# Sample attention of a hybrid encoder layer: four 32-row products on row groups of their own, scanned running sums, one turn for rotary keys

## The reference

```python
def fox_attend(q, k, v, cum_q, cum_k, qpos, kpos):
    s = jnp.einsum('bqhd,bkhd->bhqk', q, k).astype(jnp.float32) * FOX_SCALE
    s = s + jnp.swapaxes(cum_q, 1, 2)[..., :, None] - jnp.swapaxes(cum_k, 1, 2)[..., None, :]
    ...
def mla_attend(q_lat, q_rope, ckv, krope, qpos, kpos):
    s = (jnp.einsum('bqhc,bkc->bhqk', q_lat, ckv) + jnp.einsum('bqhr,bkr->bhqk', q_rope, krope)).astype(jnp.float32) * MLA_SCALE
    ...
    # sample_layer
    cum = jnp.cumsum(jnp.concatenate([c_logf.astype(jnp.float32), logf], axis=1), axis=1)
    fox_o = fox_attend(fq, k_all, v_all, cum[:, past:], cum, qpos, kpos)
```

## Time and profile before

| | us |
|---|---|
| median of 3 runs | 1612.63 (1611.25 to 1615.20) |
| profiled execution | 1609.14 |
| its span, first to last instruction | 1606.9 |
| TensorE busy in it | 1536.9 (96%) |
| VectorE, ScalarE busy | 630.9 (39%), 286.5 (18%) |
| mean granted TensorE clock | 0.988 of full speed |

### The profile page before, as it was taken

The page is one execution under the profiler, slowest core; times in us unless marked ns, Lnnn a source line. Parts: engine busy times, 40 slices in busy tenths (PEclk is TensorE's granted clock), DMA queues, the critical chain, the costliest instruction groups (busy, mean ns, idle before and its releaser), DMA issues.

```text
span 1606.9 us, 20794 instructions
## 1 busy us (share of the span) xinstructions
PE 1536.9 (96%) x7759; PEld 741.6 (46%) x7760; DVE 630.9 (39%) x1232; ACT 286.5 (18%) x617; POOL 37.7 (2%) x43
## 2 busy tenths in 40 slices
PE   6999999999999888999999999999999999999996
PEld 4876566656786563333333333333333333333332
DVE  2246444002123464344353443533533533533535
ACT  1125444210002321111111110110110110110111
POOL 0000000000004200000000000000000000000000
PEclk9999999999999979999999999999999999999999
DMA  9413145832333366399999999999999999999994
GB/s 271 134 37 111 51 196 190 286 105 96 127 105 130 114 262 243 143 403 417 417 419 417 417 419 417 417 420 417 417 420 416 418 419 416 418 419 417 418 419 201
DMA packets 125384, 481.15 MB, mean 299 GB/s; under 512 B 20048, under 2 KB 47984, under 8 KB 90400
## 3 DMA queue, kind: packets, MB, share of 16 engines
q1 hardware_dynamic: 112832, 471.79, 74.1%
q0 software_dynamic: 2016, 6.49, 1.1%
q10 hardware_dynamic: 10496, 2.32, 0.8%
HBM read 475.52 MB, written 4.65 MB: 299 GB/s over the span
## 4 chain that ended last, share of the span: by engine, by line
PE 66%; DMA 16%; SPq 11%; DVE 3%; issue 2%; ACT 1%; DVEq 0%; ACTq 0%
PE bank L463 61%; DMA ring<-in_w_gu 16%; SPq L1174 7%; SPq L1177 4%; PE bank L1092 1%; PE bank L775 1%; PE bank L1141 1%; PE bank L477 1%; PE bank L828 0%; DMA xr<-in_x_sample 0%; PE bank L786 0%; DVE small L1435 0%; PE bank L711 0%; SPq L1194 0%; DVE ring L1446 0%
## 5 line engine op out<-in xcount | busy, mean ns | idle before, releaser
L463 PE MATMUL bank<-ring,latent 128*64 128x512 f32 (+2 forms) x3328 | 745.1, 586 | 15.9 <-DMA ring<-in_w_gu 15.9
L463 PEld LDWEIGHTS bank<-ring,latent 128*64 128x64 f32 (+1 forms) x3328 | 250.7, 139 | 481.4 <-issue 413.6
L1717 DVE TENSOR_SCALAR latent<-bank 128x512 f32<-128x512 f32 x33 | 22.8, 692 | 509.8 <-PE bank L463 509.8
L1701 DVE TENSOR_TENSOR xr<-xr,bank 128x512 f32<-128x512 f32 x204 | 128.1, 683 | 44.1 <-PE bank L463 44.1
L463 PE MATMUL bank<-latent,fkT 64*128 64x512 f32 x408 | 135.0, 624 | 0.7 <-ACT latent L2054 0.7
L463 PE MATMUL bank<-hT,ring 128*128 128x384 f32 x384 | 124.5, 487 | 1.0 <-DVE hT L1328 1.0
L463 PE MATMUL bank<-ring,hT 128*128 128x256 f32 (+1 forms) x528 | 110.5, 371 | 0.0
L463 PEld LDWEIGHTS bank<-ring,hT 128*128 128x128 f32 x528 | 96.2, 190 | 13.5 <-issue 0.9
L2047 ACT ACTIVATE probTs<-latent 128x512 f32<-128x512 f32 x33 | 20.8, 630 | 455.9 <-DVE latent L1717 455.9
L463 PE MATMUL bank<-heads,latent 128*64 128x512 f32 x408 | 95.0, 601 | 1.9 <-issue 1.9
L463 PEld LDWEIGHTS bank<-hT,ring 128*128 128x128 f32 x384 | 72.8, 190 | 51.5 <-issue 1.5
(11 more groups left out here) (310 smaller groups left out, 1119.0 us busy)
## 6 DMA issues: line engine op xcount, KB each, us to landing
ring<-in_w_gu SPq DMA_DIRECT2D x256, 1024.0 KB, 19.7
ring<-in_w_down SPq DMA_DIRECT2D x128, 1024.0 KB, 21.0
ring<-in_w_in SPq DMA_DIRECT2D x16, 1024.0 KB, 11.0
ring<-in_cache_fox_k SPq DMA_DIRECT2D x8, 1024.0 KB, 4.8
ring<-in_cache_fox_v SPq DMA_DIRECT2D x8, 1024.0 KB, 7.4
ring<-in_cache_mla_ckv SPq DMA_DIRECT2D x8, 512.0 KB, 5.6
ring<-in_w_out SPq DMA_DIRECT2D x4, 1024.0 KB, 5.1
ring<-in_cache_mem_k SPq DMA_DIRECT2D x8, 512.0 KB, 3.3
```

The lines of the kernel that those rows point to most:

```text
L463: return pe.matmul(o, l, r, start=start, stop=stop, skip_group_check=True)
L1701: v.tensor_tensor(x, x, psum[5 + i % 3][:, :], ALU.add).then_inc(shares_added, 1)
L1717: v.tensor_scalar(gS, gate[:, :], LIMIT, None, ALU.min).then_inc(gate_clipped, 1)
```

## The change

- The forget product has 32 rows instead of 64: `sel4` covers 4 requests, `cumS` has two halves of 4 requests at partitions 64 to 95, and `cumN` lies apart at 96 to 127. The rotary queries are kept twice, at partitions 0 to 31 and 32 to 63.
- `sample_scores` opens four banks at once and issues the four 32-row products first, on four row groups. `("sN", b)` is split in `("sNf", b)` and `("sNm", b)`; the wait for the copy of the rotary keys comes first.
- `cumS` is made by four turns of `lgc`, interleaved by k so that a row holds the tokens in order, and two running sums on VectorE (`tensor_tensor_scan`). `cumN` takes one product with `lgsum`, which VectorE sums up before. The constant shrinks from 1024 to 384 columns. As cumS now lies in token order, the forget product reads it at every fourth word.
- The rotary keys of a request are turned once, 128x128, instead of four times 128x32, and ScalarE takes them apart in four copies of 32x128.

```diff
--- before.py
+++ after.py
@@ -55,9 +55,9 @@
 
 CONST = {}
 _at = 0
-for _name, _n in (("ident", 128), ("tri", 1024), ("blocktri", 128), ("z1", 128), ("causal", 128), ("z2", 128), ("chunk", 128),
+for _name, _n in (("ident", 128), ("tri", 384), ("blocktri", 128), ("z1", 128), ("causal", 128), ("z2", 128), ("chunk", 128),
                   ("foxnew", 240), ("mlanew", 240), ("cos", 48), ("sin", 48), ("iota", 64), ("iota1", 64), ("i64", 64),
-                  ("pmod", 1), ("pidx", 1), ("row", 1), ("neg8", 64), ("zero", 32)):
+                  ("pmod", 1), ("pidx", 1), ("row", 1), ("neg8", 64), ("neg32", 32), ("zero", 32)):
     CONST[_name] = (_at, _n)
     _at += _n
 NCONST = _at
@@ -75,7 +75,7 @@
     incl = (p[:, None] <= p[None, :]).astype(np.float32)
     strict = (p[:, None] < p[None, :]).astype(np.float32)
     put("ident", np.eye(P, dtype=np.float32))
-    put("tri", np.concatenate([strict] * 3 + [incl] * 4 + [np.ones((P, P), np.float32)], 1))
+    put("tri", np.concatenate([strict, incl, np.ones((P, P), np.float32)], 1))
     same = p[:, None] // NQ == p[None, :] // NQ
     put("blocktri", incl * same)
     put("causal", np.where(p[None, :] <= p[:, None], 0, NEG).astype(np.float32))
@@ -100,6 +100,7 @@
     put("pmod", (p % NE).astype(np.float32)[:, None])
     put("pidx", p.astype(np.float32)[:, None])
     put("row", (-(p % CAP)).astype(np.float32)[:, None])
+    put("neg32", np.concatenate([-8 * np.eye(32, dtype=np.float32)] * 4, 0))
     put("neg8", np.concatenate([-8 * np.eye(64, dtype=np.float32)] * 2, 0))
     return c
 
@@ -140,9 +141,11 @@
         xr = sb("xr", [P, NT, D])
         xflat = xr[:, :, :].rearrange("p t n -> p (t n)")
         qpair = xflat[:, 0:1024].rearrange("p (b g m) -> p b g m", b=NB, g=4)
-        qrS = xflat[0:ROPE, 1024:2048].rearrange("p (b h q) -> p b h q", b=NB, h=H)
-        cumS = xflat[64:128, 2048:2688]
-        sel8 = xflat[64:128, 1024:2048].rearrange("p (b m) -> p b m", b=NB)
+        qrS = xflat[0:2 * ROPE, 1024:2048].rearrange("p (b h q) -> p b h q", b=NB, h=H)
+        sel4 = xflat[64:128, 1024:1536].rearrange("p (b m) -> p b m", b=4)
+        cumS = xflat[64:96, 1536:2560].rearrange("p (a s) -> p a s", a=2)
+        cumN = xflat[96:128, 1536:1792].rearrange("p (a s) -> p a s", a=2)
+        lgsum = xflat[:, 3008:3072]
         logfw = xflat[:, 2944:3008]
         hT = sb("hT", [P, KD, TOK])
         fqT = sb("fqT", [P, 4, TOK])
@@ -249,8 +252,8 @@
 
         ident = cc("ident")
         t0 = CONST["tri"][0]
-        ones = con[:, t0 + 896:t0 + 1024]
-        incl_ones = con[:, t0 + 768:t0 + 1024]
+        ones = con[:, t0 + 256:t0 + 384]
+        incl_ones = con[:, t0 + 128:t0 + 384]
 
 
         bank_full = [sem(f"bank_full{i}") for i in range(8)]
@@ -568,11 +571,10 @@
             pe.wait_ge(logf_wide, 1)
             ps = open_bank(pe, "cumS")
             for k in range(KT):
-                i = mm(ps[0:64, :], lgc[:, k, :, :].rearrange("p b h -> p (b h)"), con[:, t0 + 128 * (3 - k):t0 + 128 * (3 - k) + 512], k == 0, k == KT - 1)
+                i = pe.transpose(ps[0:64, k::KT], lgc[:, k, :, :].rearrange("p b h -> p (b h)"), ident)
             done(i, "cumS")
             ps = open_bank(pe, "cumN")
-            for k in range(KT):
-                mm(ps[0:64, 0:P], lgc[:, k, :, :].rearrange("p b h -> p (b h)"), ones, k == 0, False)
+            mm(ps[0:64, 0:P], lgsum, ones, True, False)
             i = mm(ps[0:64, 0:P], logfw, cc("blocktri"), False, True)
             done(i, "cumN")
             def latent_keys(g):
@@ -786,39 +788,39 @@
                         i = pe.transpose(ps[:, P * k:P * k + P], c3[:, k, P * c:P * c + P], ident)
                     done(i, ("scT", b, c))
                 ps = open_bank(pe, ("srT", b))
-                for k in range(KT):
-                    i = pe.transpose(ps[0:ROPE, P * k:P * k + P],
-                                     ring[:, s, 1024:1152].rearrange("p (k n) -> p k n", k=KT)[:, k, :], ident)
-                done(i, ("srT", b))
+                done(pe.transpose(ps[:, 0:P], ring[:, s, 1024:1152], ident), ("srT", b))
 
             def sample_scores(b):
-                sel = sel8[:, b, :]
-                rot = qrS[:, b, :, :].rearrange("p h q -> p (h q)")
+                past, new = sel4[0:32, b % 4, :], sel4[32:64, b % 4, :]
+                rot, rot_new = (qrS[ROPE * j:ROPE * j + ROPE, b, :, :].rearrange("p h q -> p (h q)") for j in range(2))
                 lat = [qs[:, c, b, :, :].rearrange("p h q -> p (h q)") for c in range(2)]
                 for g in range(4):
                     pe.wait_ge(free(("skT", b, g)), count(("skT", b, g)))
                 if b == 0:
                     pe.wait_ge(pairs_ready, 1)
-                ps = open_bank(pe, ("sS", 2 * b))
-                mm(ps[:, :], sel, cumS[:, 0:512], True, False)
+                pe.wait_ge(free(("srT", b)), count(("srT", b)))
+                fox = open_bank(pe, ("sS", 2 * b))
+                fox_new = open_bank(pe, ("sNf", b))
+                mla_new = open_bank(pe, ("sNm", b))
+                mla = open_bank(pe, ("sS", 2 * b + 1))
+
+                mm(fox[:, :], past, cumS[:, b // 4, :].rearrange("p (s k) -> p k s", k=KT), True, False)
+                mm(mla[:, :], rot, srT[b % 2], True, False)
+                mm(fox_new[:, 0:P], new, cumN[:, b // 4, :], True, False)
+                mm(mla_new[:, 0:P], rot_new, krT[ROPE:2 * ROPE, 256:384], True, False)
                 for g in range(4):
-                    i = mm(ps[32 * g:32 * g + 32, :], qpair[:, b, g, :], skT[b % 2][:, g, :], False, True)
+                    i = mm(fox[32 * g:32 * g + 32, :], qpair[:, b, g, :], skT[b % 2][:, g, :], False, True)
                 done(i, ("sS", 2 * b))
-                ps = open_bank(pe, ("sN", b))
-                mm(ps[:, 0:P], sel, cumS[:, 512:640], True, False)
                 for g in range(4):
-                    i = mm(ps[32 * g:32 * g + 32, 0:P], qpair[:, b, g, :], fkT[:, g, 256:384], False, True)
+                    i = mm(fox_new[32 * g:32 * g + 32, 0:P], qpair[:, b, g, :], fkT[:, g, 256:384], False, True)
+                done(i, ("sNf", b))
                 for c in range(2):
-                    mm(ps[:, P:256], lat[c], ckvT[:, c, 256:384], False, False)
-                i = mm(ps[:, P:256], rot, krT[0:ROPE, 256:384], False, True)
-                done(i, ("sN", b))
+                    i = mm(mla_new[:, 0:P], lat[c], ckvT[:, c, 256:384], False, c == 1)
+                done(i, ("sNm", b))
                 for c in range(2):
                     pe.wait_ge(free(("scT", b, c)), count(("scT", b, c)))
-                pe.wait_ge(free(("srT", b)), count(("srT", b)))
-                ps = open_bank(pe, ("sS", 2 * b + 1))
                 for c in range(2):
-                    mm(ps[:, :], lat[c], scT[b % 2][:, c, :], c == 0, False)
-                i = mm(ps[:, :], rot, srT[b % 2], False, True)
+                    i = mm(mla[:, :], lat[c], scT[b % 2][:, c, :], False, c == 1)
                 done(i, ("sS", 2 * b + 1))
 
             def sample_turn(n):
@@ -1383,7 +1385,9 @@
                 dve.wait_ge(logit_exp, t + 1)
                 v.scalar_tensor_tensor(logf[:, t, :], lz[:, t, :], 0.0, lln[:, t, :], ALU.min, ALU.subtract).then_inc(logf_ready, 1)
             dve.wait_ge(logf_ready, NT)
-            v.tensor_copy(logfw.rearrange("p (b h) -> p b h", b=NB), bc(logf[:, 2:3, :], [P, NB, H])).then_inc(logf_wide, 1)
+            v.tensor_copy(logfw.rearrange("p (b h) -> p b h", b=NB), bc(logf[:, 2:3, :], [P, NB, H]))
+            dve.wait_ge(lgc_loaded, 16 * KT)
+            v.tensor_reduce(lgsum, lgc.rearrange("p k b h -> p (b h) k"), X, ALU.add).then_inc(logf_wide, 1)
             for c in range(2):
                 ps = take(("qcT", c))
                 give(v.tensor_scalar(qcT[:, c, :], ps[:, 0:TOK], gq_c[:, c:c + 1], None, ALU.mult), ("qcT", c))
@@ -1392,9 +1396,14 @@
             v.tensor_copy(cumT[0:H, :], ps[0:H, 0:256])
             give(v.tensor_copy(cumT[64:64 + H, :], ps[0:H, 0:256]), "cumP")
             ps = take("cumS")
-            give(v.tensor_copy(cumS[:, 0:512], ps[0:64, :]), "cumS")
+            for a in range(2):
+                r = slice(32 * a, 32 * a + 32)
+                last = v.tensor_tensor_scan(cumS[:, a, :], ps[r, :], bc(cc("zero")[r, 0:1], [32, 512]), 0.0, ALU.add, ALU.add)
+            give(last, "cumS")
             ps = take("cumN")
-            give(v.tensor_copy(cumS[:, 512:640], ps[0:64, 0:P]), "cumN")
+            for a in range(2):
+                last = v.tensor_copy(cumN[:, a, :], ps[32 * a:32 * a + 32, 0:P])
+            give(last, "cumN")
             for t in range(NT):
                 ps = take(("qr", t))
                 rope(ps[:, 0:256].rearrange("p (h r) -> p h r", r=ROPE), qrope[:, t, :, :], t, H, qrope_ready, ("qr", t))
@@ -1406,16 +1415,17 @@
             dve.wait_ge(zeroed, 2)
             dve.wait_ge(free(("fqT", 3)), count(("fqT", 3)))
```

(25 more changed lines are left out.)

## The result

| | before | after |
|---|---|---|
| median of the runs, us | 1613.91 (1611.25 to 1615.38, 4 runs) | 1604.80 (1602.80 to 1605.37, 4 runs) |
| ratio, 95% interval | | 0.9943 (0.9926 to 0.9961) |
| profiled execution, us | 1609.14 | 1604.64 |
| its span, us, and mean granted clock | 1606.9, 0.988 | 1602.5, 0.980 |
| one steady pass of the batch loop, us | 14.90 | 13.13 |

A forecast was written before the change was run, and what follows sets the result against it. TensorE was taken to bound the kernel ahead of a rigid expert tail. Running sums -3.6, pass 0 +0.1, scores -7 x 2.38 and turns -6 x 0.33 gave -22.2 us: 1612.63 to 1590.4 us, range 1586 to 1601.

The forecast's parts named there:

- Bound and tail: Whole kernel: TensorE sets the pace ahead of the expert stage, a rigid tail that moves by whatever TensorE gains.
- Running sums: Once, ahead of the batch loop: TensorE work falls from 4.67 to 1.06 us, 3.6 us less, no cost taken for VectorE.
- Price of the four-product section: Score section: four 32-row products side by side take 1.08 us instead of 2.92; with regrouping, 2.38 us less a pass.
- rival A: Forget product: reading cumS at every fourth word costs 1.02 us more a pass, 8.2 us back, 1598.6 us; chance 0.18.
- Rival B: Score section: the row groups don't overlap, 2.33 us instead of 1.08, 10 us back, 1600.4 us; chance 0.08 including two by two.
- One turn for rotary keys: Batch loop: one turn for four saves 0.33 us in each of 6 passes; ScalarE's 0.47 us more is covered.
- Pass 0 "loses 0.1 us and gains nothing": First pass: scores start 1.2 us later, save 2.4, then copies cost 1.0, by the sum about 0.1 us lost.
- Waits in passes 1 to 7: Batch loop: no new waits take over; the tightest cover, for the next cache keys, is 0.7 us.
- rival C: Passes 1 to 7: cache keys land in 7 us instead of 4.8, 10 us back, 1601 us; chance 0.06.
- The base: Whole kernel: profiled execution 1609.14 us; the gain was applied to the median of 1612.63 us, 3.5 us above it.
- The range: Whole kernel: 1586 to 1601 us, the high end set to include A and B; likeliest case alone 1586 to 1595.

The follow-up runs named there:

- e5: The kernel before, unedited, run again for a second trace: 1613.80 us, span 1612.4 us.
- e2: The change with cumS copied into key order by VectorE, so the forget product reads it contiguously: 1595.45 us, ratio 0.9894.
- e1: The change run again with nothing edited: 1604.03 us, ratio 0.9943.
- e13: The change with the forget product reading cumS at another step in each pass: one trace, score section 4.20 us at every second word, 5.07 at every fourth.
- e8: e2 with the rotary keys turned four times and copied once by ScalarE, as in the kernel before: 1593.00 us, ratio 0.9872.
- e7: e2 with the 40-column forget projections taken in turns with the 256-column key-value ones: 1593.29 us, ratio 0.9875.
- e10: e8 with e7's mixing of the 40-column and 256-column projections: 1591.82 us.
- e9: The change, strided read kept, with the rotary keys turned four times and copied once as before: 1603.67 us, ratio 0.9944.
- e4: e2 with the four 32-row products back at their old places, one after the other: 1619.65 us.
- e6: e2 with the rotary-key turn ahead of the latent turns and its four copies ahead of the last latent copy: 1593.34 us.
- e11: e6 with e7's mixing of the 40-column and 256-column projections: 1590.29 us, ratio 0.9856.
- e3: e2 with the running sums made by the old products on the big constant, already in contiguous order: 1601.05 us.

## Why the prediction was wrong, step by step

Where the time went, from the second trace of before (e5) to the trace of after, by the starts of the pieces and of the sections:

| stretch | forecast, us | traces, us |
|---|---|---|
| start of the first projections (18.52, 19.33) | 0 | +0.8 |
| first projections and running sums | -3.6 | -3.55 |
| up to the turns ahead of pass 0 (50.45, 50.46) | 0 | 0.0 |
| passes 0 and 1 (33.42, 37.01) | +0.1 - 2.4 - 0.3 = -2.6 | +3.6 |
| five steady passes (74.53, 65.68) | 5 x -2.71 = -13.6 | -8.85 |
| last pass | -2.4 | -1.5 |
| sum | -22.2 | -9.5 |

**Bound and tail: right.** TensorE sets the pace ahead of the expert stage, and the whole tail moved by what TensorE gained.

**Running sums: right.** Timeline of TensorE after, to set beside the earlier trace rows:

```profile
96.36 0.63 PE L574 MATMUL bank<-con,heads 128*64 128x128 f32 x4
96.92 0.65 PE L466 MATMUL bank<-con,xr 128*64 128x128 f32 x4
97.50 1.35 PE L466 MATMUL bank<-ring 128*128 128x256 f32 x5
```

1.14 us for 1.06 forecast. The four turns that write every fourth word of a bank take 0.56 us with their change of shape, where 0.43 was taken: at most 0.1 us extra. VectorE's sum took 0.59 us (0.5 taken), the two scans 2.44 us where up to 7 were allowed for, and no TensorE row waits for any of them.

**Price of the four-product section: wrong, one of the two large misses.** The step that failed is "they cost the longest, 2 x 512 x 0.83 = 0.85": the price of a column came from contiguous reads, and the strided one went into rival A with a chance of 0.18. A column took 0.97 us / 512 = 1.89 ns, almost what rival A had borrowed from VectorE (1.86). A said 8.2 us back, 1.02 in all eight passes; e2 against e1 measured 8.6. That the totals are so close is partly luck: 5.9 to 6.6 us of it are the read (0.9 in six passes, little in the two at low clock), the rest low clock elsewhere. The reason set against A, that the reduction's price holds the overhead of short sums, was weaker than the agreement it was set against. The Trainium skill ("Advanced Engine Details and Errata", Memory Cachelines) gives 16-byte lines in SBUF and asks for at least two hits on a line; e13 agrees at each step: 8 bytes 4.20 us, 16 bytes 5.07, 32 bytes and more 5.0 to 5.1. It should have made A the forecast. Its neighbour, the Trainium skill's speed-up of 3.07 for four products ("TensorE: Matmul & The Clock Gate", Part 3, Measured speedup vs the span model), an estimated 1.37 us here, is not borne out for this section: 1.06 us in e2. Two of its four products have only 128 columns, so no run tests four of 512. Rival B is out.

**One turn for rotary keys: wrong, the gain of 2 us is not there.** The 0.33 us a steady pass is there (12.22 against 12.55 us), and so are the cover in a steady pass (four copies 1.06 us, 1.04 forecast) and no wait. In passes 0 and 1 there is no cover, and the prediction priced that as the length of the copies alone. From the turns ahead of pass 0 to the chain's score piece of pass 2, pair by pair: 37.15 us in e2 and 31.76 in e8; 36.11 in e7 and 32.36 in e10; 37.54 in the change and 34.35 in e9. 3.2 to 5.4 us are lost in these single traces against 2.0 gained in the other passes. The medians are 2.4, 1.5 and 0.4 to 1.1 us lower without this part; by the ratios, which take out the session, it is 3.5, 1.9 and nothing. In each pair the ranges touch. So the forecast gain of 2 us is not there, a loss is likely with contiguous sums, and with the strided ones none is shown.

**Pass 0 "loses 0.1 us and gains nothing": wrong.** With pass 1 it makes the other large miss: +3.6 us in the table where -2.6 was forecast, 6.2 us. Two terms failed. First, the delays of the scores were 1.84 us ahead of pass 0 and 1.68 ahead of pass 1, where the sum had 1.2 and 1.04: 1.3 us more, most of it the 0.4 to 0.6 us between the last copy's end and the first MATMUL, which it left out. Second, it was worked out at 2.4 GHz. The longer waits for ScalarE stand ahead of stretches at 1.2 GHz: the whole score section of pass 1 took 7.52 us instead of 5.45, that of pass 0 6.84. Together 3.5 us, in products that the sum had at full speed. The strided read is in these 5.45 us.

That the waits bring the low clock rests on all the traces. Seven versions or repeats have waits of 2.0 and 2.5 to 2.6 us (the change, e1 to e4, e7, e13), and 168 to 204 us at 0.73 to 0.88. Five have 1.2 to 1.3 and 1.8 to 2.2 us (e6, e8 to e11), and 0.91 to 0.98. But e10 and e11 still have a low clock in pass 1 (passes 0 and 1 of e11 take 34.43 us, e6's 31.03), so a short wait is no guarantee, and what decides is open.

**Waits in passes 1 to 7 (rival C): right that there are none.** The cache keys land in 4.8 us as before, and behind pass 1 TensorE's only waits in the sample attention are the 2.6 us at its end that before has too.

**The base: misread.** The forecast took the profiled execution's stretches as those of the median. Its time was 3.5 us under the median, and the granted clock of 60 to 86 us shows where: e5's first projections take 71.03 us, its 67.69. Of the 5.5 us between the two spans 3.6 lie ahead of the gate projections and the rest behind. Since the sum was applied to the median, this cost the forecast nothing, but the first comparison of traces showed 4.4 us of gain instead of 9.9, and nearly a wrong cause: the low clock at 64 us looked like the change's doing until e5.

**The range.** It reached to rival A or rival B alone, at 1601. What happened is A together with a loss in passes 0 and 1 that had been given 0.1 us. In the table the misses are 6.2 us in passes 0 and 1, 5.6 in the passes behind them and 0.8 at the start. Independent misses have to be added before a high end is set.

**What stays open.** No edit touches the work from the start of the gate projections to the first of the equal expert blocks (27.80 us each), and yet it takes 341.9 to 346.4 us in the fifteen traces, with other stretches of low clock in each; e3's trace loses 4.4 us to e2's there, more than its running sums cost. So a difference of a few us between two traces is read only within the stretch that was edited. What a stretch of low clock at one place does to the next: each version has them at other places, and 1 to 2 us between medians go with it unexplained: e11's pass 1 is at 1.2 GHz where e6's is not, and e11 is the faster by 3.1 us, one more than the mixing gives elsewhere.

## What to carry to other kernels

Price a moving operand by its step as well as by its columns, and lay out what several products read so that the many reads are contiguous and the one write or copy pays: here one VectorE pass of permuting copies, off the critical path, bought 8.6 us in the median, some 6 of them seen in the passes themselves. Look at the first and last rounds of a loop by themselves: an edit that moves work to an engine with cover in the steady state can lose as much or more in the two rounds without cover as it gains in the six with it. Take a second trace of the kernel before, and compare traces only after their granted clocks.

## What the runs showed of the hardware

- A 32-row fp32 product whose moving operand steps by 16 to 256 bytes takes 0.93 to 1.03 us for each 512-column MATMUL (0.97 us, 1.89 ns a column, at 16 bytes); contiguous or at 8-byte steps 0.53 to 0.56 us start to start. All were read beside three other row groups; none was run alone. At the 1.2 GHz level the strided one takes no longer: in pass 1 above, its MATMULs start at 187.82, 188.86 and the next section at 189.86, just like the contiguous rotary ones beside them (187.82, 188.84). At that level the two cost the same. e13's contiguous forget product at that level, in pass 1, has starts at 187.68 and 188.66 and the next section at 189.68.
- Four 32-row products on four row groups (two of 512 and two of 128 columns) cost what the longest costs: 1.06 us in e2, and 1.97 us in the change, where one slow member holds the section.
- Toward the end of a run of 40-column products, or just behind it, the granted clock falls to the 1.2 GHz level for some 3 to 7 us, with TensorE recorded as busy throughout (26.00 of 26.00 us from 60 to 86 us, at 0.87 in seven traces and 0.93 in two). It is there in nine of the eleven traces with these products in a row (not in the first trace of before and in e9's) and in none of the four in which they are taken in turns with 256-column ones. The medians put it at 1.2 to 3.1 us.
